# The finest recurrence level without differences and with factors copied into PSUM; low parts of the recurrence's weight tiles half on VectorE

## The chip, the cores and the metric

One NeuronCore of one Trainium2 chip runs the whole program. The time is the device time of one execution in microseconds (us). The engines are TensorE (PE), VectorE (DVE), ScalarE (ACT), GpSimd (POOL) and SyncE (SP, which issues DMA). Each takes its instructions in order; they wait for each other through semaphores.

## The reference

Two layers on 512 tokens of width 1024, all in float32: a latent attention (layer 0) and a gated linear recurrence (layer 1, `_hgrn2`), each followed by an expert layer (`_peer`) that takes most of the time. The change concerns the recurrence alone:

```python
f = lb + (1.0 - lb) * jax.nn.sigmoid(f_pre.astype(jnp.float32))
log_f = jnp.log(f)
k = 1.0 - f
...
b = jnp.cumsum(lfc, axis=2)
o_inter = jnp.einsum('bhtd,bhde->bhte', qc * jnp.exp(b), state)
diff = b[:, :, :, None, :] - b[:, :, None, :, :]
decay = jnp.where(causal, jnp.exp(jnp.where(causal, diff, 0.0)), 0.0)
a = jnp.einsum('bhtd,bhsd,bhtsd->bhts', qc, kc, decay)
o_intra = jnp.einsum('bhts,bhse->bhte', a, vc)
...
o = o * lax.rsqrt(jnp.mean(o * o, axis=-1, keepdims=True) + NORM_EPS)
o = o.reshape(B, S, E) * out_norm.astype(jnp.float32) * jax.nn.silu(g_pre.astype(jnp.float32))
```

There are 8 heads (128 channels each). The output of a head is normed, so its sign can be set back in the gain that follows.

## The kernel before

**The stream of weights.** All weights pass as tiles of 128 x 1024 through a ring of 4 slots (`RING`). SP loads a tile to `w_raw`. ScalarE rounds it to `w_hi` (`high`, L700), and the rest `w_raw - w_hi` goes to `w_lo`: by POOL (`lows`, L612) or by VectorE (`low`, L1389), as `low_by_dve` says. Before the change VectorE makes low parts only in the expert layers. A product of weights and activations is three matmuls (`three`, L1640 to L1642: high x high, and the two with a low part); PE waits for a tile's low part with `wait_low`. The tiles concerned are `hg_g` 0 to 7 (gate projection, one for each head) and after them `hg_out` 0 to 7 (output projection); `hg_g` + 8 is `hg_out` 0.

**The recurrence.** The 512 steps are worked on in 4 chunks of 128. Inside a chunk the decayed product of queries and keys is split into 8 levels: level 0 is the diagonal, and level p = 1 to 7 pairs blocks of m = 128 >> p steps with the blocks beside them; in level 7 m is 1. For each head h there are 8 slots k, so n = 8h + k runs from 0 to 63, and every engine has a loop over n:

- POOL (`take_diff`): the differences of the cumulated log decay against a block's edge, into one of two buffers `diff`. L646 in slot 0, L651 in slots 1 to 7. In slot 0 `head_roots(h - 2)` (L663, L666) follows, and low parts (L612) at n = 6, 9, 11, 16, 24, 32, 40, 48, 56, the last three for `hg_out` 0 to 2. After the loop come `head_roots` 6 and 7 and the low part of `hg_out` 3.
- ScalarE (`level_exp`): exponentials of the differences into one of two PSUM banks (`scaling`), L971 in slot 0, L976 (keys) and L977 (queries) in the others. Between them: the copy of the transposed keys `kdT` (L1016) and `next_high` (L700) in slot 5, the gate's tanh (L951) in slot 4, squares (L983) in slot 6, `head_scaled` (L991) in slot 1, the decay (L963) after slot 7.
- VectorE (`scale_level`): keys and queries times these factors (L1489 in slot 0; L1499, L1500 else) into `xx`, also two buffers. `mask_level` (L1511, L1519) takes PE's result of two slots before out of PSUM. Then `gate_silu` (L1538), `gated` (L1544), `states` (L1528, L1530) and q times decay (L1568) in slot 7. Head 7 has three `gated_low` (L1551) besides.
- PE follows the list `recurrence()`: per head level 0 (L1941), the transposes of the decayed keys (`kd`, L1925), levels 1 to 7 (L1939), the chunk states (`st`, L1950) after level 3, which need `kdT`, the transposes `turn` (L1958), 8 parts of a gate tile (three matmuls each) strewn between, and values and output of the head before (L1985, L1994) after level 1. A level waits for `xx` and for the mask step that frees its PSUM bank (two are in turn). After the last head: parts of the output projection in the order `hg_out` 0 and 1 (all by L1640 to L1642), then 2 and 3, then `turn` 7.

In level 7 both key and edge are the same step, so the key's factor is exp(0) = 1 and the query's is f itself, computed by difference and exponential.

## Time and profile before

| | us |
|---|---|
| median of 3 runs | 2929.11 |
| lowest, highest | 2926.78, 2932.37 |
| the profiled execution | 2927.46 |
| its span (first to last instruction) | 2925.2 |
| PE busy | 2893.8 |
| VectorE busy | 2364.2 |
| POOL busy | 1285.6 |
| ScalarE busy | 1194.7 |
| recurrence, level 0 of head 0 to the end of head 7 | 1550.68 to 1661.63 |

The busy times are of the whole program; the recurrence is under 4% of it. A busy PE includes matmuls that overlap one another, so short waits between them may not be seen as idle time. Times of rows are from the start of the span. What ended an idle time is inferred from semaphores.

### The profile page before, as it was taken

The numbers are of one execution on the slowest core, as the hardware profiler recorded it, in microseconds if no ns is written. First come the engines' busy times: TensorE is split into PE (matmuls) and PEld (weight loads), VectorE is DVE, ScalarE is ACT, GpSimd is POOL, SyncE is SP. The second block draws the span as 40 slices with busy tenths as digits, with TensorE's granted clock in tenths as the row PEclk, the third lists the DMA queues.
The fourth block names the chain that finished last, engine by engine and source line by source line (L and its number), as shares of the span: only waits on it lengthen the run. The fifth ranks groups of instructions, "written<-read, shape, count | busy, mean of one in ns | idle before, by whom it ended". The sixth has DMA issues, their size and how long they took to land.

```text
span 2925.2 us, 43270 instructions
## 1 busy us (share of the span) xinstructions
PE 2893.8 (99%) x15746; PEld 2581.3 (88%) x15746; DVE 2364.2 (81%) x4466; ACT 1194.7 (41%) x1928; POOL 1285.6 (44%) x764
## 2 busy tenths in 40 slices
PE   8999999999999999999999999999999999999998
PEld 7678999999998888888887788999999998888887
DVE  7537999999878888888356758999998978888887
ACT  6543334444433333333436543334444433333333
POOL 4133565334444444442348643664334444444441
PEclk9999999999999999999999999999999999999999
DMA  4122568999999999998321032669999999999995
GB/s 152 37 100 90 165 183 311 367 377 363 372 379 398 361 362 361 359 357 320 107 95 57 30 116 91 199 197 366 365 379 351 381 396 378 361 358 364 360 362 212
DMA packets 346146, 799.96 MB, mean 273 GB/s; under 512 B 27984, under 2 KB 192080, under 8 KB 345680
## 3 DMA queue, kind: packets, MB, share of 16 engines
q1 hardware_dynamic: 235200, 478.32, 47.2%
q0 software_dynamic: 73728, 268.47, 24.1%
q10 hardware_dynamic: 37008, 50.41, 4.7%
q8 instruction: 127, 2.08, 0.3%
q14 instruction: 83, 0.68, 0.1%
HBM read 694.33 MB, written 102.76 MB: 272 GB/s over the span
## 4 chain that ended last, share of the span: by engine, by line
PE 94%; POOL 2%; ACT 2%; DVE 1%; issue 0%; DMA 0%; DVEq 0%; SPq 0%; ACTq 0%
PE PS L1640 29%; PE PS L1642 29%; PE PS L1641 29%; PE PS L1861 3%; PE PS L1840 1%; POOL w_lo L612 1%; POOL arena L651 1%; PE PS L1770 1%; PE PS L1771 1%; PE PS L1817 1%; DVE resid L1114 1%; ACT arena L713 0%; ACT PS L976 0%; ACT PS L977 0%; PE PS L1805 0%
## 5 line engine op out<-in xcount | busy, mean ns | idle before, releaser
L700 ACT ACTIVATE w_hi<-w_raw 128x1024 fp32r<-128x1024 f32 x607 | 641.4, 1058 | 758.2 <-PE PS L1642 691.1
L1640 PE MATMUL PS<-x_hi,w_hi 128*128 128x384 f32 (+1 forms) x2564 | 897.5, 350 | 0.0
L1642 PE MATMUL PS<-x_hi,w_lo 128*128 128x384 f32 (+1 forms) x2564 | 886.3, 346 | 0.0
L1641 PE MATMUL PS<-x_lo,w_hi 128*128 128x384 f32 (+1 forms) x2564 | 885.2, 345 | 0.0
L1640 PE MATMUL PS<-w_hi,x_hi 128*128 128x512 f32 x1744 | 679.7, 390 | 1.7 <-POOL w_lo L612 0.9
L1642 PE MATMUL PS<-w_hi,x_lo 128*128 128x512 f32 x1744 | 678.6, 389 | 0.0
L1641 PE MATMUL PS<-w_lo,x_hi 128*128 128x512 f32 x1744 | 678.5, 389 | 0.0
L623 POOL DMA_INDIRECT arena<-in_v_t,arena x256 | 427.0, 1668 | 557.4 <-DVE resid L1412 527.5
L612 POOL TENSOR_TENSOR w_lo<-w_raw,w_hi 128x1024 fp32r<-128x1024 f32 x167 | 414.7, 2489 | 493.3 <-ACT w_hi L700 493.2
L1389 DVE TENSOR_TENSOR w_lo<-w_raw,w_hi 128x1024 fp32r<-128x1024 f32 x440 | 536.6, 1219 | 97.1 <-ACT w_hi L700 92.0
L623 POOL DMA_INDIRECT arena<-in_u_rows,arena x256 | 363.9, 1421 | 509.9 <-DVE arena L1396 455.6
L1642 PEld LDWEIGHTS PS<-x_hi,w_lo 128*128 128x128 f32 x2564 | 481.2, 188 | 21.2
L1641 PEld LDWEIGHTS PS<-x_lo,w_hi 128*128 128x128 f32 x2564 | 481.8, 188 | 18.3 <-issue 0.5
L1640 PEld LDWEIGHTS PS<-x_hi,w_hi 128*128 128x128 f32 x2564 | 481.7, 188 | 17.7 <-issue 0.5
L1640 PEld LDWEIGHTS PS<-w_hi,x_hi 128*128 128x128 f32 x1744 | 327.4, 188 | 70.5 <-POOL w_lo L612 1.3
L1641 PEld LDWEIGHTS PS<-w_lo,x_hi 128*128 128x128 f32 x1744 | 327.4, 188 | 68.0
L1642 PEld LDWEIGHTS PS<-w_hi,x_lo 128*128 128x128 f32 x1744 | 327.4, 188 | 68.0
L871 ACT ACTIVATE arena<-PS 128x384 f32<-128x384 f32 x256 | 125.9, 492 | 639.5 <-PE PS L1642 631.3
L1412 DVE SCALAR_TENSOR_TENSOR resid<-arena,resid 128x1024 f32<-128x1024 f32 x256 | 327.1, 1278 | 1.3
L1396 DVE SCALAR_TENSOR_TENSOR arena<-arena 128x1024 f32<-128x1024 f32 x256 | 306.9, 1218 | 0.4
L1429 DVE TENSOR_TENSOR x_lo<-arena,x_hi 128x384 fp32r<-128x384 f32 x256 | 144.6, 565 | 165.8 <-ACT x_hi L902 160.1
L1423 DVE TENSOR_TENSOR arena<-arena 128x384 f32<-128x384 f32 x256 | 141.0, 551 | 2.9 <-DMA arena<-acts_dram 2.9
(203 smaller groups left out, 2314.1 us busy)
## 6 DMA issues: line engine op xcount, KB each, us to landing
w_raw<-in_u_t SPq DMA_DIRECT2D x256, 512.0 KB
w_raw<-in_v_t SPq DMA_DIRECT2D x256, 512.0 KB
acts_dram<-arena ACTq DMA_DIRECT2D x256, 192.0 KB
gates_dram<-arena SPq DMA_DIRECT2D x24, 2048.0 KB
arena<-acts_dram SPq DMA_DIRECT2D x256, 192.0 KB
arena<-gates_dram SPq DMA_DIRECT2D x64, 768.0 KB
w_raw<-in_hg_t SPq DMA_DIRECT2D x40, 512.0 KB
w_raw<-in_pq_t SPq DMA_DIRECT2D x32, 512.0 KB
```

What stands on the lines that cost most here:

```text
L612: pool.tensor_tensor(w_lo[:, n % RING, :], w_raw[:, n % RING, :], f32(w_hi[:, n % RING, :]), ALU.subtract).then_inc(pool_low, 1)
L623: pool.indirect_dma_start(row[k % ROWS], None, u_at if k < HK else v_at, bass.IndirectOffsetOnAxis(ap=at, axis=0))\
L700: act.activation(w_hi[:, slot, :], w_raw[:, slot, :], ACT.Copy).then_inc(hi_ready, 1)
L871: act.activation(act_st[:, c % RING, :], PS[:, c % 4, 0:D], ACT.Gelu).then_inc(gelu_done, 1)
L1389: dve.tensor_tensor(w_lo[:, n % RING, :], w_raw[:, n % RING, :], f32(w_hi[:, n % RING, :]), ALU.subtract).then_inc(dve_low, 1)
L1396: dve.scalar_tensor_tensor(r, r, 1.0, far_x, ALU.mult, ALU.mult, accum_out=far_act[:, k:k + 1]).then_inc(sem("dotted"), 1)
L1412: dve.scalar_tensor_tensor(resid[:, FAR, :], r, far_w[:, k:k + 1], resid[:, FAR, :], ALU.mult, ALU.add).then_inc(sem("far_added"), 1)
L1423: dve.tensor_tensor(product[:, c % RING, :].rearrange(tokens, t=HALF_TOK), act_ld[:, c % RING, :].rearrange(tokens, t=HALF_TOK), gate_ld[: ...
L1429: dve.tensor_tensor(product_at(x_lo, c), product[:, c % RING, :].rearrange("p (t n) -> p t n", n=P), product_at(f32(x_hi), c), ALU.subtrac ...
L1640: pe.matmul(ps, wh, xh, start=start, stop=False)
L1641: pe.matmul(ps, wh, xl, start=False, stop=False)
L1642: return pe.matmul(ps, wl, xh, start=False, stop=stop)
```

## The change

Level 7 (slot 7) no longer uses a difference or an exponential. The kernel keeps k with its sign turned, gk = f - 1. ScalarE copies gk into the PSUM bank of factors, keys' and queries' part. VectorE copies the keys' part to `xx`, and makes the queries' part as (factor + 1) x q, which is f x q. The turned sign passes through the head's output and is set back by a negative gain. POOL's loop takes 7 differences a head instead of 8; the buffers of `diff` alternate by 7h + k. In head 0 ScalarE copies `kdT` in slot 3 instead of slot 5. The low parts of `hg_g` 3, 5, 7 and of `hg_out` 1 are made by VectorE in slots n = 11, 27, 43, 59; POOL makes those of `hg_g` 2, 4, 6 and `hg_out` 0 at n = 8, 20, 36, 44, and that of `hg_out` 2 after the loop, behind both `head_roots`. The function `low` is moved out of `experts`, unchanged.

```diff
@@ -132,6 +132,8 @@
 def low_by_dve(n):
 
 
+    if BASE["hg_g"] <= n < BASE["pq1"]:
+        return n - BASE["hg_g"] in (3, 5, 7, 9)
     return any(BASE[f"u{k}"] + FIRST_DVE_LOW <= n < BASE[f"v{k}"] + NKEYS for k in range(2))
 
 
@@ -637,9 +639,9 @@
             def take_diff(n):
 
 
-                h, k = divmod(n, 8)
+                h, k = divmod(n, LEVELS)
                 if n >= 2:
-                    pool.wait_ge(sem("level_exp"), n - 1)
+                    pool.wait_ge(sem("level_exp"), (n - 2) // LEVELS * 8 + (n - 2) % LEVELS + 1)
                 d = diff[:, n % 2, :]
                 half, b = SEQ // 2, gb[:, h, :]
                 if k == 0:
@@ -668,17 +670,18 @@
             pool.wait_ge(sem("cumulated"), HEADS)
             pool.memset(minus_half, -0.5).then_inc(sem("exponent_made"), 1)
             pool.wait_ge(sem("exponent_made"), 1)
+            low_at = {8: 2, 20: 4, 36: 6, 44: 8}
             for n in range(8 * HEADS):
-                take_diff(n)
-                if n % 8 == 0 and n >= 16:
-                    head_roots(n // 8 - 2)
-                if n in (6, 9, 11):
-                    lows(BASE["hg_g"] + n // 3, BASE["hg_g"] + n // 3 + 1) if n < 11 else                         lows(BASE["hg_g"] + RING, BASE["hg_g"] + RING + 1)
-                elif n >= 16 and n % 8 == 0:
-                    lows(BASE["hg_g"] + RING + n // 8 - 1, BASE["hg_g"] + RING + n // 8)
+                h, k = divmod(n, 8)
+                if k < LEVELS:
+                    take_diff(LEVELS * h + k)
+                if k == 0 and h >= 2:
+                    head_roots(h - 2)
+                if n in low_at:
+                    lows(BASE["hg_g"] + low_at[n], BASE["hg_g"] + low_at[n] + 1)
             head_roots(HEADS - 2)
             head_roots(HEADS - 1)
-            lows(BASE["hg_out"] + RING - 1, BASE["u1"] + FIRST_GATHER)
+            lows(BASE["hg_out"] + 2, BASE["u1"] + FIRST_GATHER)
             gathers(1)
 
 
@@ -964,15 +967,20 @@
 
             def level_exp(n):
                 h, k = divmod(n, 8)
-                act.wait_ge(sem("level_diff"), n + 1)
                 scaling_used(act, n - 2)
-                d = diff[:, n % 2, :]
+                d = diff[:, (LEVELS * h + k) % 2, :]
+                if k < LEVELS:
+                    act.wait_ge(sem("level_diff"), LEVELS * h + k + 1)
                 if k == 0:
                     act.activation(scaling(n), d, ACT.Exp).then_inc(sem("level_exp"), 1)
                     return
 
                 m = P >> k
                 by_part = scaling(n).rearrange("p (w s b m) -> p w s b m", w=2, s=2, m=m)
+                if k == LEVELS:
+                    act.activation(by_part[:, 0], level_keys(gk[:, h, :], m), ACT.Copy)
+                    act.activation(by_part[:, 1], level_queries(gk[:, h, :], m), ACT.Copy).then_inc(sem("level_exp"), 1)
+                    return
                 act.activation(by_part[:, 0], level_keys(d, m), ACT.Exp, scale=-1.0)
                 act.activation(by_part[:, 1], level_queries(d, m), ACT.Exp).then_inc(sem("level_exp"), 1)
 
@@ -1011,10 +1019,11 @@
                 for k in range(8):
                     if 8 * h + k >= 2:
                         level_exp(8 * h + k)
-                    if k == 5:
+                    if k == (5 if h else 3):
                         ready(act, ("kd", h))
                         free(act.activation(kdT.rearrange("p a b -> p (a b)"), PSb(("kd", h)), ACT.Copy),
                              ("kd", h))
+                    if k == 5:
                         if h < HEADS - 1:
                             next_high(BASE["hg_g"] + h)
                     if k == 6 and h >= 1:
@@ -1106,6 +1115,12 @@
                     free(dve.scalar_tensor_tensor(x_lo[:, c, :], PSb(("xT", k, c)), gain[:, g:g + 1],
                                                   f32(x_hi[:, c, :]), ALU.mult, ALU.subtract),
                          ("xT", k, c))
+
+            def low(n):
+
+                dve.wait_ge(hi_ready, n + 1)
+                dve.tensor_tensor(w_lo[:, n % RING, :], w_raw[:, n % RING, :], f32(w_hi[:, n % RING, :]),
+                                  ALU.subtract).then_inc(dve_low, 1)
 
             def add_to_resid(name, t):
                 for n in (2 * t, 2 * t + 1):
...
@@ -1461,12 +1470,12 @@
             norm(2, "v0")
 
             out_gain = gain[:, G_AT["out"]:G_AT["out"] + HEADS]
-            chain(dve.tensor_scalar(out_gain, out_gain, 0.5 * P ** 0.5, None, ALU.mult))
+            chain(dve.tensor_scalar(out_gain, out_gain, -0.5 * P ** 0.5, None, ALU.mult))
             for h in range(HEADS):
                 was_freed(dve, ("hg_f", h))
                 chain(dve.tensor_scalar(gb[:, h, :], gb[:, h, :], lbt[:, 3, h:h + 1], lbt[:, 1, h:h + 1],
                                         ALU.mult, ALU.add))
-                chain(dve.tensor_scalar(gk[:, h, :], gb[:, h, :], -1.0, 1.0, ALU.mult, ALU.add))
+                chain(dve.tensor_scalar(gk[:, h, :], gb[:, h, :], 1.0, None, ALU.subtract))
                 dve.tensor_scalar(gb[:, h, :], gb[:, h, :], SMALLEST_F, None, ALU.max)\
                    .then_inc(sem("forget"), 1)
             dve.wait_ge(sem("mask_in"), 16)
@@ -1496,6 +1505,12 @@
                 factor = d.rearrange("p (w s b m) -> p w s b m", w=2, s=2, m=m)
                 keys = xx[:, x % 2, 0:SEQ // 2].rearrange("p (b s m) -> p s b m", s=2, m=m)
                 queries = xx[:, x % 2, SEQ // 2:SEQ].rearrange("p (s b m) -> p s b m", s=2, m=m)
+                if k == LEVELS:
+                    dve.tensor_copy(keys, factor[:, 0])
+                    dve.scalar_tensor_tensor(queries, factor[:, 1], 1.0,
+                                             level_queries(gq[:, h, :], m), ALU.add, ALU.mult)\
+                        .then_inc(sem("level_x"), 1)
+                    return
                 dve.tensor_tensor(keys, level_keys(gk[:, h, :], m), factor[:, 0], ALU.mult)
                 dve.tensor_tensor(queries, level_queries(gq[:, h, :], m), factor[:, 1], ALU.mult)\
                    .then_inc(sem("level_x"), 1)
@@ -1551,6 +1566,7 @@
                 dve.tensor_tensor(x_lo[:, h, :], gq[:, h, :], f32(x_hi[:, h, :]), ALU.subtract)\
                    .then_inc(sem("gated_low"), 1)
 
+            low_in_slot = {11: 3, 27: 5, 43: 7, 59: 9}
             for n in range(8 * HEADS):
                 h, k = divmod(n, 8)
                 if k == 0 and n >= 2:
@@ -1569,6 +1585,8 @@
                        .then_inc(sem("q_decayed"), 1)
                 if k == 5 and h >= 2:
                     gated(h - 2)
+                if n in low_in_slot:
+                    low(BASE["hg_g"] + low_in_slot[n])
                 if (h, k) in ((7, 1), (7, 3), (7, 5)):
                     gated_low(k // 2)
             mask_level(8 * HEADS - 2)
```

## Rows read from the trace of the kernel before

**Rows 1.** The page: busy us of each engine (share of the span) x instructions.

```profile
PE 2893.8 (99%) x15746; PEld 2581.3 (88%) x15746; DVE 2364.2 (81%) x4466; ACT 1194.7 (41%) x1928; POOL 1285.6 (44%) x764
```

**Rows 2.** PE's waits in the whole span: total us, times, longest us.

```profile
PE PS L1950 <- ACT arena L1016: 2.7, 2, 1.4
```

**Rows 3.** Stages by head (0, 1, 3, 7): length, busy PE PEld DVE ACT POOL, clock.

```profile
1550.68:1563.49 12.81, 11.11 (x72) 9.53 (x70) 10.24 (x23) 6.11 (x15) 10.08 (x7) 1.00 0.13 43
1563.49:1578.24 14.75, 12.77 (x84) 11.15 (x85) 12.73 (x29) 7.98 (x25) 13.59 (x12) 1.00 0.23 75
...
1592.13:1605.98 13.85, 13.66 (x90) 11.48 (x89) 11.86 (x30) 9.65 (x31) 12.31 (x12) 1.00 0.14 40
...
1647.47:1661.63 14.16, 11.97 (x79) 9.98 (x80) 13.34 (x31) 9.99 (x35) 8.57 (x9) 1.00 0.10 36
```

**Rows 4.** Timeline of PE in head 3: start, us, what.

```profile
1601.38 0.60 PE L1939 MATMUL PS<-arena 128*128 128x128 f32 x4
1601.74 0.48 PE L1640 MATMUL PS<-x_hi,w_hi 128*128 128x512 f32 x1
...
1602.29 0.40 PE L1642 MATMUL PS<-x_hi,w_lo 128*128 128x512 f32 x1
1602.76 0.71 PE L1939 MATMUL PS<-arena 128*128 128x128 f32 x4
```

**Rows 5.** Timeline of POOL, end of head 3 and start of head 4.

```profile
1602.31 2.39 POOL L612 TENSOR_TENSOR w_lo<-w_raw,w_hi 128x1024 fp32r<-128x1024 f32 x1
1604.65 3.56 POOL L651 TENSOR_TENSOR arena<-arena 128x512 f32<-128x512 f32 x3
1608.61 4.10 POOL L651 TENSOR_TENSOR arena<-arena 128x512 f32<-128x512 f32 x4 [0.39 <-ACT PS L977]
```

**Rows 6.** Timeline of ScalarE, levels 1, 2 and 5 of head 4, then kdT.

```profile
1606.19 0.39 ACT L976 ACTIVATE PS<-arena 128x256 f32<-128x256 f32 x1 [3.13 <-POOL arena L651]
...
1607.82 0.40 ACT L976 ACTIVATE PS<-arena 128x256 f32<-128x256 f32 x1
...
1610.85 0.38 ACT L976 ACTIVATE PS<-arena 128x256 f32<-128x256 f32 x1
...
1611.46 0.58 ACT L1016 ACTIVATE arena<-PS 128x512 f32<-128x512 f32 x1
```

**Rows 7.** Timeline of VectorE in head 4.

```profile
1606.91 0.42 DVE L1499 TENSOR_TENSOR arena<-arena,PS 128x256 f32<-128x256 f32 x1 [0.50 <-ACT PS L977]
...
1607.59 0.73 DVE L1519 COPY_PREDICATED arena<-mask_bits,PS 128x256 f32<-128x256 uint16 x1
...
1611.90 0.42 DVE L1499 TENSOR_TENSOR arena<-arena,PS 128x256 f32<-128x256 f32 x1 [0.97 <-PE PS L1939]
```

**Rows 8.** Timeline of ScalarE and PE in head 0.

```profile
1551.57 0.60 PE L1925 MATMUL PS<-const,arena 128*128 128x128 f32 x4
...
1554.50 0.60 ACT L951 ACTIVATE arena<-PS 128x512 f32<-128x512 f32 x1 [3.41 <-PE PS L1642]
...
1555.61 0.59 ACT L1016 ACTIVATE arena<-PS 128x512 f32<-128x512 f32 x1
...
1556.34 0.91 PE L1950 MATMUL PS<-arena 128*128 128x128 f32 x6 [1.43 <-ACT arena L1016]
```

**Rows 9.** POOL and VectorE in head 1; lines L1389, L1528: ns min/median/max.

```profile
1574.62 2.38 POOL L612 TENSOR_TENSOR w_lo<-w_raw,w_hi 128x1024 fp32r<-128x1024 f32 x1
...
1575.05 2.50 DVE L1568 TENSOR_TENSOR arena<-arena 128x512 f32<-128x512 f32 x1
...
L1389 DVE TENSOR_TENSOR w_lo<-w_raw,w_hi x440: 1212/1218/1246, 454.2 to 2904.1; 128x1024 fp32r<-128x1024 f32 x147
...
L1528 DVE COPY arena<-PS x8: 275/281/303, 1558.8 to 1658.3; 128x128 f32<-128x128 f32 x8
```

**Rows 10.** Timeline after head 7, POOL and PE.

```profile
1669.18 2.38 POOL L612 TENSOR_TENSOR w_lo<-w_raw,w_hi 128x1024 fp32r<-128x1024 f32 x1
...
1671.61 0.50 PE L1640 MATMUL PS<-w_hi,x_hi 128*128 128x512 f32 x1 [0.88 <-POOL w_lo L612]
```

More of the change, by code:

```diff
@@ L1384, in make_onehots @@
                        .then_inc(onehots, 1)
-                def low(n):
-                    dve.wait_ge(hi_ready, n + 1)
-                    dve.tensor_tensor(w_lo[:, n % RING, :], w_raw[:, n % RING, :], f32(w_hi[:, n % RING, :]),
-                                      ALU.subtract).then_inc(dve_low, 1)
                 def far_dot(k):
```

## Prediction

> **What bounds the kernel now.** I read the page's busy line first: TensorE (PE) is busy for 2893.8 of 2925.2 us [rows 1], so nearly all of the program is a TensorE stream that this change doesn't touch. The waits of PE come next: the largest entry inside the recurrence is L1950's for ScalarE's kdT copy, 2.7 us in two waits [rows 2]. The change leaves PE's instructions as they are. It can move only the time in which PE waits in the recurrence.
>
> That time is found with a table of stages, cut where PE starts level 0 of a head (L1941) [rows 3]. Head 0 takes 12.81 us, head 1 14.75, head 3 13.85 (heads 2 to 6, five of them, differ by under 0.1), head 7 14.16, all at a granted clock of 1.00. A modelled PE row hides short waits, so I compare starts. A level group (L1939) that is not waited for starts 0.36 us before the next 512-column matmul (1601.38 to 1601.74). The matmul at 1602.29 should hand over after 0.23 us, but the next L1939 starts at 1602.76, 0.47 later, and needs 0.47 instead of 0.36 us itself [rows 4]. So a wait costs 0.24 + 0.11 us and no idle is shown. Walking one steady head (1592.13 to 1605.98) this way gives 0.38 at level 1, 0.35 at level 6, and 0.33 in four small ones, 1.06 us together: PE's floor for a head is 12.8 us. Five steady heads hold 5.3 us; the shown idle of heads 0, 1, 7 and the tail, with the hidden part ahead of each, about 10 more. Some 16 us (0.5%) is the most that any change of this kind could win.
>
> What PE waits for in a steady head is a ring of engines. POOL works off a low part (2.39 us) and then the differences [rows 5]. ScalarE's exponential of level 1 waits 3.13 us for the first of these [rows 6]; VectorE then waits 0.50 us for ScalarE before it scales level 1, and masks level 7 of the head before at 1607.59 (0.73 us), which frees PE's bank for level 1. It waits again, 0.97 us at 1611.90, for PE's level 2 [rows 7]. From there to the next level 0 VectorE runs without a break but for drains, so it is the second bound, 0.50 us behind POOL.
>
> **The change, part by part.** (a) POOL loses the level-7 difference of each head (1.03 us, from four in 4.10 [rows 5]) and four of its low parts at 2.39. It also issues the others elsewhere: at slots 8, 20, 36, 44 instead of right ahead of each head's level-1 difference. In a head with no low part the 3.13 us wait goes, VectorE's 0.50 goes with it, and the mask of level 7 comes early enough for PE's 0.38 to go. Next late is VectorE's unbroken stretch, and PE's level 6 wait stays. A steady head without a POOL low part (3 and 6) therefore gains 0.4 to 0.5: 0.95 for both.
>
> (b) Head 0: ScalarE copies kdT at level 3 instead of after level 5, ahead of the gate's tanh. The copy is at 1555.61 now, behind the tanh, which ScalarE reaches after 3.41 us of idle, and PE's L1950 starts at 1556.34, after 1.43 of idle of its own. The transposes that the copy needs end at 1552.2 (1551.57 + 0.60) [rows 8], so it can end at 1552.8, and PE can take L1950 straight after level 3. It isn't free: ScalarE now stands at kd(0) until 1552.2 with a tile's high part and the exponential of level 4 queued behind it. The latter ended at 1551.1 (the tanh's start less its idle) and now ends at about 1554.4; the 3.41 us absorb it. VectorE takes level 4 half a microsecond later, and PE needs that only after L1950, so the cover holds. I take 1.5 us here, and 0.25 for the product of q and the decay, which in heads 0 and 1 is blocked behind a POOL low part (2.50 us in head 1 [rows 9]; free it should be under 0.7, since twice its size takes 1.22, below): 1.75.
>
> (c) Head 1 has three low parts of POOL in or just ahead of it now, and none after. It loses the blocked 2.50, the late exponential behind it and the second L1950 wait; walked through at the row times it ends at PE's floor of 12.55 (no turn(h-2) in it): gain 2.2.
>
> (d) Heads 2, 4, 5 carry a POOL low part between the differences of levels 4 and 5. In a steady head's times, ScalarE's second exponential frees the buffer at 1607.82 + 0.7, some 1.3 earlier after (a), so at 1607.2. POOL would then do difference 4 until 1608.35, the low part until 1610.75 and difference 5 until 1611.8. The exponential of level 5, at 1610.85 now, comes at 1612.0, and the kdT copy behind it on ScalarE, at 1611.46 now, at 1612.6 [rows 6]. PE's L1950 waits for that copy with everything of PE queued behind it. That costs 1.15 against now, of which later slack gives back most of 0.8: each of these heads is 0.35 to 0.4 longer than now, 1.1 for three. Were the exponential not late it would be -0.4 each, were the low part fully on the path +1.6: the ends are -1.2 and +4.8.
>
> (e) VectorE gets four low parts, at level 3 of heads 1, 3, 5, 7. One takes 1.22 us (440 rows of the same operation [rows 9]). In heads 1 and 3 it sits where VectorE waits 0.97 for PE now, and 1.3 after (a), so the wait hides it: nothing. In head 5 it meets POOL's low part and waits for it, 0.3. Head 7 has no such wait, since three gated_low steps fill it: +1.2, less 0.5 from (a) and 0.2 that PE gives back: +0.5. If that cover fails altogether each costs up to 1.2, and up to 1.0 more behind a difference of POOL.
>
> (f) Level 7: ScalarE's two exponentials become two copies of 256 columns from the same strides. No row has a copy of that shape into PSUM; the nearest are the 256-column exponential at 0.39 us and kdT's copy, 0.58 for 512 columns, so 0.29 to 0.39 [rows 6]. I take 0.39, no change; ScalarE is not the bound. On VectorE the key product becomes a copy from PSUM. L1528, 128 columns, takes 0.281 against 0.42 for 256 columns in L1499 [rows 9, 7], so by size 256 cost the same; at best 0.14 x 8 = 1.1 us of VectorE go. I take nothing. The sign of k is carried through and cancelled in the gain: same instructions.
>
> (g) The tail. Today the low part of hg_out tile 2 is made at slot 56, in head 7, and only tile 3's is made after head_roots(7): POOL's at 1669.18 for 2.38, and PE's first matmul of tile 3 starts at 1671.61, 0.88 idle [rows 10]. After the change both stand behind head_roots(7), which waits for the last head's squares. Tile 2's is ready at 1671.6, tile 3's at 1673.95. PE, in order, stops at 1669.2 for 2.4 us, does 1.4 us of tile 2, and stops again. Tile 3 starts at 1674.0 instead of 1671.6: +2.4. Nothing else of PE can pass, and DMA loads behind the two tiles have over 5 us of slack.
>
> **The sum.** -1.75 - 2.2 - 0.95 + 1.1 (heads 2, 4, 5) + 0.3 + 0.5 + 2.4 = -0.6 us. The profiled execution took 2927.46 us, 2.26 more than its span; it becomes 2926.9. The median of the runs lies 1.65 above it, so 2928.5. A measurement of this kernel can tell some 0.2%, 5.9 us, from no change.
>
> One rule speaks against (e). The row shows VectorE's product with two SBUF sources at 2.50 us, ending 0.5 after a POOL low part that had begun 0.43 before it [rows 9]. The Trainium skill (SBUF — State Buffer, Who interferes with whom) says that such an instruction and a GpSimd one that reads SBUF share a port pair as an exclusive lock: the later one is blocked until the first ends. By that rule, the trace agrees, every new VectorE low part can block a difference or be blocked by one; this is the price of up to 1.0 in (e).
>
> **The rivals.** *The collision of (d) takes the place of the old wait* (slower side): the exponential of level 5 is late by the whole low part. Price: 4.8 instead of 1.1, and 2 more where VectorE's low parts block or wait for differences: 2928.5 + 3.7 + 2 = 2934. It decides when (d) and (e) exceed the 3.95 of (b) and (c) less the tail's 2.4. For: POOL has one pair of buffers, so difference 5 can't run ahead. Against: POOL has 3 us of slack per head after (a). To be over +0.2% it must also lose head 0's gain.
>
> *The gain of (a) reaches every head*: the late difference is hidden by VectorE's stretch, heads 2, 4, 5 gain 0.4. Sum -0.6 - 2.3 - 0.3 = -3.2: 2925.9. For: VectorE takes level 5 only behind level 4 (1611.90 [rows 7]), a mask and the gate. Against: PE's L1950 waits for the copy behind that exponential, wherever VectorE is.
>
> *Head 0 doesn't gain*, since ScalarE stands at kd(0) and its queue comes late: +1.5, 2930.0.
>
> *The tail doesn't cost* (tile 2 is covered by something I don't see): -2.4, 2926.1; with the rival above 2923.5. Against: the order of POOL is plain in the code.
>
> **How the numbers follow.** Forecast 2928.5 as it stands, chance 0.45; the second rival 0.14; head 0 0.14; no tail cost 0.07; the collision 0.20, of which 0.09 beyond +0.2%. The bounds of (d) alone reach from -2.3 to +3.7 around the forecast; with the 2.8 us by which the runs of the kernel before lie around their median, of which about 1.5 stay in a median (2926.2 - 1.5, 2932.2 + 1.5), the range is 2924.7 to 2933.7. Within 0.2% of before (2923.3 to 2935.0): 0.86. Faster: 0.05, mostly the second and fourth rivals together. Slower: 0.09, the far part of the collision.
>
> **What the profile would show.** Right: no wait of ScalarE for POOL at level 1; L1950 of head 0 near 1554.7; head 1 under 13 us; heads 3 and 6 at 13.3 to 13.5; PE idle before L1950 in heads 2, 4, 5; and in the tail two L1640 waits for POOL's low parts, 2.2 and 0.9 us. Wrong: the even heads no longer than the odd ones, VectorE low parts above 1.3 us, or hg_out tile 2 not waited for. The prediction falls if PE's idle in the recurrence shrinks by over 6 us or grows.

## The result, and the profile after

The changed kernel takes 2932.6 us (median; 2929.8 to 2938.8), the kernel before 2929.1. The ratio is 1.0013, with a 95% interval of 1.0007 to 1.0019: 3.5 us slower, by 2.1 to 5.6. That is inside the range (2924.7 to 2933.7) and inside the 0.2% that I gave 0.86, but I had forecast 0.6 us faster, and the interval excludes that. 4.1 us have to be found. The wide upper side of the range came from the bounds of (d); (d) kept its forecast and other things filled that space, so the hit of the range is luck.

The page of after says nothing of it. Its busy line, as [rows 1] for before:

```profile
PE 2893.0 (99%) x15746; PEld 2583.2 (88%) x15746; DVE 2368.6 (81%) x4470; ACT 1195.5 (41%) x1928; POOL 1264.6 (43%) x752
```

POOL lost 21 us and 12 instructions (8 differences, 4 low parts), VectorE gained 4 instructions and 4 us, PE is as busy as before. The stages show more. The table of stages of after, cut where PE starts level 0 of a head (line L1959 now); the columns are those of [rows 3]; the last line goes from turn 6 to turn 7 (L1976), which is the tail:

```profile
1549.94:1561.69 11.75, 11.27 (x71) 9.60 (x70) 9.57 (x23) 7.27 (x16) 7.71 (x6) 1.00 0.13 45
1561.69:1574.65 12.96, 12.81 (x84) 11.30 (x85) 12.78 (x30) 9.87 (x31) 9.58 (x10) 1.00 0.14 42
1574.65:1588.96 14.31, 13.06 (x90) 11.53 (x89) 12.16 (x30) 9.89 (x31) 11.17 (x11) 1.00 0.12 39
1588.96:1602.43 13.47, 13.36 (x89) 11.44 (x89) 13.08 (x31) 9.87 (x31) 9.13 (x10) 1.00 0.13 39
1602.43:1616.77 14.34, 13.07 (x89) 11.58 (x88) 12.18 (x30) 10.03 (x32) 11.23 (x11) 1.00 0.11 38
1616.77:1633.62 16.85, 14.62 (x90) 13.10 (x90) 14.64 (x33) 10.38 (x33) 12.04 (x11) 0.90 0.20 64
1633.62:1646.95 13.33, 11.73 (x80) 9.71 (x78) 10.63 (x28) 9.85 (x31) 8.29 (x9) 1.00 0.00 1
1646.95:1661.82 14.87, 12.13 (x80) 10.03 (x80) 14.56 (x32) 8.62 (x30) 5.55 (x6) 1.00 0.13 36
1661.82:1675.57 13.75, 10.89 (x54) 8.60 (x55) 3.81 (x6) 5.16 (x17) 5.90 (x4) 1.00 0.16 46
```

Beside before and beside what the steps of the prediction come to (us):

| | h0 | h1 | h2 | h3 | h4 | h5 | h6 | h7 | tail | sum |
|---|---|---|---|---|---|---|---|---|---|---|
| before | 12.81 | 14.75 | 13.89 | 13.85 | 13.86 | 13.82 | 13.81 | 14.16 | 11.47 | 122.4 |
| by my steps | 11.06 | 12.55 | 14.3 | 13.35 | 14.2 | 14.5 | 13.35 | 14.7 | 13.87 | 121.9 |
| after | 11.75 | 12.96 | 14.31 | 13.47 | 14.34 | 16.85 | 13.33 | 14.87 | 13.75 | 125.6 |

The recurrence became 3.2 us longer, nearly all of the 3.5. Six of the nine stages are within 0.2 us of my steps, heads 0 and 1 fall short by 0.7 and 0.4 us of gain, and head 5 alone is 2.35 us too long. It is also the only line whose clock column isn't 1.00.

PE's waits from the first level 0 to turn 7 of after (total us, times, longest), those over 0.5 in total:

```profile
PE PS L1968 <- ACT arena L1024: 4.8, 3, 2.2
PE PS L1957 <- DVE arena L1534: 3.1, 5, 0.9
PE PS L1658 <- POOL w_lo L614: 2.9, 2, 2.2
PE PS L1959 <- DVE arena L1534: 1.0, 2, 0.5
```

The wait for kdT was 2.7 us in two waits, in heads 0 and 1 [rows 2]; now it is 4.8 in three, and these are heads 2, 4 and 5: the change has moved the wait and made it longer. The wait for POOL's low parts in the tail went from 0.88 [rows 10] to 2.9. Added up, PE's shown waits over these stages grew from 8.2 to 12.3 us.

Two of the signs that I had named as speaking against me are there: PE's idle grew, and all four of VectorE's low parts took over 1.3 us (1.58, 1.58, 1.90 and 1.41). The signs for me are there too: L1968 of head 0 came 4.07 us after level 0 (1554.01), head 1 took 12.96, heads 3 and 6 took 13.47 and 13.33, PE idled before L1968 in heads 2, 4 and 5, and twice in the tail. Most of the walk through the heads was right.

**Head 5.** Timeline of VectorE, POOL, ScalarE and PE of after in head 5:

```profile
1620.65 1.90 DVE L1122 TENSOR_TENSOR w_lo<-w_raw,w_hi 128x1024 fp32r<-128x1024 f32 x1
...
1619.10 2.38 POOL L614 TENSOR_TENSOR w_lo<-w_raw,w_hi 128x1024 fp32r<-128x1024 f32 x1
1621.43 3.02 POOL L653 TENSOR_TENSOR arena<-arena 128x512 f32<-128x512 f32 x2
...
1623.55 0.39 ACT L984 ACTIVATE PS<-arena 128x256 f32<-128x256 f32 x1 [2.70 <-POOL arena L653]
...
1624.18 0.58 ACT L1024 ACTIVATE arena<-PS 128x512 f32<-128x512 f32 x1
...
1624.90 0.91 PE L1968 MATMUL PS<-arena 128*128 128x128 f32 x6 [2.23 <-ACT arena L1024]
...
1627.95 0.63 PE L1660 MATMUL PS<-x_hi,w_lo 128*128 128x512 f32 x1
1628.38 0.63 PE L1658 MATMUL PS<-x_hi,w_hi 128*128 128x512 f32 x1
```

Read it from the top. VectorE's low part starts at 1620.65 while POOL's (1619.10 to 1621.48) is under way and takes 1.90 us instead of 1.22. It is still running when POOL comes to its differences, and these two take 3.02 instead of 2.04 (heads 2 and 4). So the exponential of level 5 waits 2.70 us, kdT comes behind it at 1624.18, and PE stands for 2.23 us. So far this is my step (d) with (e) on top. Then comes what I had not thought of: PE's matmuls of 512 columns, which start 0.23 us apart elsewhere, start 0.43 apart. The stages around that place, columns as above:

```profile
1622.67:1624.90 2.23, 0.00 (x1) 0.03 (x1) 2.10 (x6) 1.35 (x4) 2.23 (x3) 1.00 0.60 125
...
1626.00:1629.30 3.30, 3.30 (x13) 2.81 (x12) 2.53 (x7) 3.02 (x13) 1.76 (x3) 0.50 0.28 109
1629.30:1633.62 4.32, 4.32 (x27) 3.76 (x26) 3.61 (x9) 2.27 (x8) 2.63 (x3) 1.00 0.01 2
```

The granted clock is 0.50, the lower level of 1.2 GHz, in the stretch from 1626.0 to 1629.3, about 1 us behind the end of the idle of 2.23 us; up to 1625.5 and from 1629.3 on it is 1.00, which is 2.4 GHz. The profile of before has no such place in the recurrence.

**The tail.** Timeline of POOL and PE of after behind head 7:

```profile
1669.34 4.68 POOL L614 TENSOR_TENSOR w_lo<-w_raw,w_hi 128x1024 fp32r<-128x1024 f32 x2
...
1671.74 0.50 PE L1658 MATMUL PS<-w_hi,x_hi 128*128 128x512 f32 x1 [2.20 <-POOL w_lo L614]
1674.07 0.50 PE L1658 MATMUL PS<-w_hi,x_hi 128*128 128x512 f32 x1 [0.66 <-POOL w_lo L614]
```

Here I was right: both low parts stand behind `head_roots`, PE stops twice, and turn 7 comes at 1675.57 instead of 1673.10.

### The profile page after: what moved, and what is told of

Same layout as the page of the kernel before. It is cut to its first block, busy times and chain, and to the rows that moved or that the text cites. A ratio compares the mean times of both kernels' runs of the same rounds, so it can differ in the third digit from the quotient of the medians.

```text
span 2929.1 us, 43254 instructions
## 1 busy us (share of the span) xinstructions
PE 2893.0 (99%) x15746; PEld 2583.2 (88%) x15746; DVE 2368.6 (81%) x4470; ACT 1195.5 (41%) x1928; POOL 1264.6 (43%) x752
## 4 chain that ended last, share of the span: by engine, by line
PE 95%; DVE 2%; ACT 1%; POOL 1%; issue 1%; DMA 0%; DVEq 0%; SPq 0%; ACTq 0%
PE PS L1658 29%; PE PS L1660 29%; PE PS L1659 29%; PE PS L1879 3%; PE PS L1858 1%; PE PS L1788 1%; PE PS L1835 1%; PE PS L1789 1%; DVE resid L1129 1%; POOL w_lo L614 0%; ACT arena L716 0%; PE PS L1957 0%; DVE arena L1534 0%; PE PS L1823 0%; PE PS L1668 0%
## 5 line engine op out<-in xcount | busy, mean ns | idle before, releaser
L1122 DVE TENSOR_TENSOR w_lo<-w_raw,w_hi 128x1024 fp32r<-128x1024 f32 x444 | 543.4, 1224 | 100.0 <-ACT w_hi L703 93.5
L614 POOL TENSOR_TENSOR w_lo<-w_raw,w_hi 128x1024 fp32r<-128x1024 f32 x163 | 404.8, 2488 | 492.8 <-ACT w_hi L703 492.7
```

The source lines that it names most:

```text
L614: pool.tensor_tensor(w_lo[:, n % RING, :], w_raw[:, n % RING, :], f32(w_hi[:, n % RING, :]), ALU.subtract).then_inc(pool_low, 1)
L1122: dve.tensor_tensor(w_lo[:, n % RING, :], w_raw[:, n % RING, :], f32(w_hi[:, n % RING, :]), ALU.subtract).then_inc(dve_low, 1)
```

## The experiments

The theories: (T1) the loss sits in the POOL low part between the differences of levels 4 and 5, in head 5 in its meeting with VectorE's, and in the tail; what remains of the change wins. (T2) The half clock in head 5 is a loss of its own that follows PE's idle. (T3, rival) Something that the whole change brings, the copies into PSUM or VectorE's four low parts, costs everywhere, and its place in head 5 is chance. All kernels below compute the whole result. For each the stages of its profile are given as in the table above.

**The changed kernel again.** No edit.

> The changed kernel once more, unaltered, timed and profiled. Two theories of why it is about 3.5 us slower than before. Theory 1 (a collision and the clock): in head 5 VectorE's low part in slot 43 and POOL's in slot 44 block each other, difference 5 comes late, PE idles 2.2 us and then runs 3.4 us at half its clock, so head 5 takes 16.9 us instead of 13.8. Then a second profile shows PE's L1968 of head 5 again waiting over 2 us; the half clock shows again if the idle alone causes it. Theory 2 (the low parts of VectorE cost as such): head 5's length is work on VectorE, and the clock was a chance of that one profile; then head 5 comes out near 14.5 to 15.5 here. The tail's wait for POOL (2.2 and 0.7 us) is the same in both. Time against before: 1.0005 to 1.0015 by theory 1, 1.000 to 1.0008 by theory 2.

Stages: 11.74 12.95 14.31 13.47 14.34 16.88 13.34 14.86, tail 13.76. Not one differs from after by over 0.03 us, the half clock in head 5 included. Time 2930.45 against 2928.59, ratio 1.0007 (0.9998 to 1.0016). So stages can be compared to a tenth of a microsecond between single profiles of the recurrence, while the time of a whole run can't be told to 2 us.

**POOL's low part of head 5 three slots later.**

```diff
-low_at = {8: 2, 20: 4, 36: 6, 44: 8}
+low_at = {8: 2, 20: 4, 36: 6, 47: 8}
```

> The changed kernel, POOL's low part of hg_out 0 moved from slot 44 to slot 47, where no difference of this head stands behind it. Theory 1: the collision is gone, ScalarE's kdT copy comes in time, PE doesn't idle before L1968 in head 5, the clock stays at full and head 5 takes 13.3 to 13.6 us instead of 16.9: 3.3 us less than the changed kernel, about level with before. Theory 2 (VectorE's own 1.2 us is what costs): head 5 stays over 14.5 us and the gain is under 1 us.

Head 5 takes 13.49 instead of 16.85, all other stages are the same to 0.1. Time 2927.92, ratio 0.9997 (0.9988 to 1.0006). One tile's low part in one slot was worth 3.4 us. In this head of that kernel the two engines still get in each other's way, POOL and then VectorE:

```profile
1622.13 3.35 POOL L614 TENSOR_TENSOR w_lo<-w_raw,w_hi 128x1024 fp32r<-128x1024 f32 x1
...
1621.67 1.59 DVE L1122 TENSOR_TENSOR w_lo<-w_raw,w_hi 128x1024 fp32r<-128x1024 f32 x1
```

3.35 instead of 2.38 and 1.59 instead of 1.22, and PE has no shown wait in the whole head. So a meeting as such need not cost PE anything. I read it so that what decides is whether a difference that somebody waits for stands behind the two.

**VectorE's low part of head 5 two slots earlier.**

```diff
-low_in_slot = {11: 3, 27: 5, 43: 7, 59: 9}
+low_in_slot = {11: 3, 27: 5, 41: 7, 59: 9}
```

> The changed kernel, VectorE's low part of hg_g 7 moved from slot 43 to slot 41, before POOL's low part begins in slot 44, which stays. Theory 1: head 5 becomes like heads 2 and 4, which have a POOL low part alone: 14.3 us, PE idles about 1.3 us before L1968, the clock stays at full; 2.5 us less than the changed kernel. Theory 2: VectorE does the same work, so head 5 stays near its length of the unaltered kernel. If the half clock comes with 1.3 us of idle too, head 5 takes about 16 us.

I had expected head 5 to become like heads 2 and 4 (14.3). It takes 15.33. POOL, then VectorE, in this head of that kernel:

```profile
1619.66 3.35 POOL L614 TENSOR_TENSOR w_lo<-w_raw,w_hi 128x1024 fp32r<-128x1024 f32 x1
...
1618.90 1.89 DVE L1122 TENSOR_TENSOR w_lo<-w_raw,w_hi 128x1024 fp32r<-128x1024 f32 x1
```

VectorE's now meets a difference first (1.89) and then holds up POOL's low part (3.35). So the collision was moved, not avoided. PE's wait before L1968 is 1.62 instead of 2.23 us, with 0.30 one level earlier, and head 5 keeps the full clock. In this kernel it falls in the tail instead, after the wait of 2.20 us there, and the tail takes 14.49 instead of 13.75. Time 2930.22, ratio 1.0009 (1.0000 to 1.0018).

**The tail as before: POOL makes hg_out 2 in slot 55.**

```diff
-low_at = {8: 2, 20: 4, 36: 6, 44: 8}
+low_at = {8: 2, 20: 4, 36: 6, 44: 8, 55: 10}
...
-            lows(BASE["hg_out"] + 2, BASE["u1"] + FIRST_GATHER)
+            lows(BASE["hg_out"] + 3, BASE["u1"] + FIRST_GATHER)
```

> The changed kernel, POOL's low part of hg_out 2 made in slot 55 (head 6) instead of behind both head_roots. The tail as in the prediction: from turn 6 to turn 7 PE takes 11.5 us instead of 13.75, the 2.2 us wait for a POOL low part goes and one of 0.9 us stays, 2.3 us less than the changed kernel. The rival: PE's time in the tail is bound by turn 7's chain, and the wait moves to another place: less than 1 us is won.

The tail takes 11.46, so the 2.3 us are this one tile's place. But head 6 takes 14.30 instead of 13.33. In slot 55 POOL waits 1.83 us for ScalarE's high part, and its first differences of head 7 come late by that and by the low part (1644.92). VectorE's product of q and the decay (1645.99) meets them and takes 1.54 us instead of the 0.68 of after, and level 0 of head 7 waits 1.38 us for the mask behind it. That one place gives back 1.0 of the 2.3 us. Time 2929.14, ratio 1.0002 (0.9993 to 1.0011).

This kernel also bears on T2. The edit lies behind head 5, which has the same code, the same collision and the same idle, and keeps its clock. Timeline of PE:

```profile
1626.70 0.91 PE L1968 MATMUL PS<-arena 128*128 128x128 f32 x6 [2.24 <-ACT arena L1024]
1627.44 0.60 PE L1976 MATMUL PS<-const,arena 128*128 128x128 f32 x4
```

The stage of the 3 us behind it, columns as above:

```profile
1627.88:1630.85 2.97, 2.97 (x19) 2.59 (x18) 2.48 (x7) 2.95 (x13) 1.49 (x3) 1.00 0.16 65
```

Head 5 takes 15.35 with the full clock and 16.85 and 16.88 with the half clock, in front of the same work. From L1968 to the second L1957 behind it, it is 3.01 us here (1626.70 to 1629.71) and 4.60 in after (1624.90 to 1629.50). So the 3.0 us that head 5 lost against before are 0.5 from POOL's low part (as heads 2 and 4), 1.0 from the collision and 1.5 from the clock.

**All of POOL's low parts in slot 7** (n = 23, 39, 47), in two series on two chips.

```diff
-low_at = {8: 2, 20: 4, 36: 6, 44: 8}
+low_at = {8: 2, 23: 4, 39: 6, 47: 8}
```

> The changed kernel with POOL's low parts of hg_g 4 and 6 and hg_out 0 in slot 7 of their heads (n = 23, 39, 47) instead of slot 4 (20, 36, 44). Theory: a POOL low part between differences 4 and 5 makes difference 5, the kdT copy and so L1968 of PE late. Heads 2 and 4, 14.3 us with it, then take about 13.5 us, as head 5 did once its low part stood in slot 47; L1968 isn't waited for. 1.7 us less than the run with slot 47 alone. The rival: heads 2 and 4 are long because head 3's pace is handed on (even heads have no VectorE low part, so something else is late); then they stay over 14 us.

> The kernel with all POOL low parts in slot 7 once more, unaltered, beside the mended one on the same chip. In its first profile the clock fell in the tail and in the expert layer though no wait there was longer than in the changed kernel. Theory: which stretch falls varies from execution to execution, the lengths of heads 0 to 7 do not (11.75, 12.96, 13.4 to 13.46 for heads 2 to 6, 14.86). The rival: the fall is tied to the program; then the tail is 14.6 us again and the expert layer falls in the same place.

Heads 2 to 6 all take 13.40 to 13.47. Against after that is -0.9, -0.9 and -3.4 us in heads 2, 4 and 5. Heads 3 and 5, with a low part on VectorE (1.58 us each), take 13.44 to 13.47, heads 2, 4 and 6 without one 13.40 to 13.47. Times 2926.81 (ratio 0.9996, 0.9987 to 1.0005) and 2926.23 (0.9989, 0.9980 to 0.9998). In both profiles the clock falls in the tail, in or right behind the wait of 2.2 us. I had expected the place of a fall to change from one execution to the next; the fall in the tail came again, a second one in an expert layer did not. Stages of the second one's tail:

```profile
1664.30:1666.50 2.20, 0.01 (x1) 0.00 (x0) 0.00 (x0) 1.02 (x4) 2.20 (x2) 1.00 0.00 0
1666.50:1669.90 3.40, 3.38 (x8) 2.69 (x9) 0.00 (x0) 0.00 (x0) 2.29 (x1) 0.52 0.47 164
```

It costs only 0.6 us there (14.37 against 13.77 with the same wait and the full clock, in the kernel with slot 47), and 0.8 in the first profile (14.60): PE, at half speed, reaches the second tile when its low part is ready, so the wait of 0.66 us isn't paid besides.

**Level 7 without differences, alone.** The kernel before, with the level-7 part of the change only (7 differences a head, the two copies on ScalarE, the COPY and (factor + 1) x q on VectorE, the turned sign).

```diff
-                take_diff(n)
+                if n % 8 < LEVELS:
+                    take_diff(LEVELS * (n // 8) + n % 8)
...
+                if k == LEVELS:
+                    act.activation(by_part[:, 0], level_keys(gk[:, h, :], m), ACT.Copy)
+                    act.activation(by_part[:, 1], level_queries(gk[:, h, :], m), ACT.Copy).then_inc(sem("level_exp"), 1)
+                    return
```

> The kernel before with the level-7 part of the change alone: seven differences a head, copies into PSUM, the turned sign; low parts and the kdT copy as before. Theory: POOL's ring was only 0.50 us longer than VectorE's, and 1.03 us go from it, so each of heads 2 to 6 falls to 13.4 to 13.5 us without any low part moved; 2 to 2.5 us less than before in all, ratio about 0.9992. The rival: the low part right before difference 1 is what made it late, and dropping a difference behind it helps nothing: heads stay at 13.8.

Stages: 12.36 14.18 13.93 13.91 13.91 13.89 13.87 14.21, tail 11.44. Time 2928.96, ratio 1.0001 (0.9992 to 1.0010). My theory of 13.4 to 13.5 falls and its rival holds: steady heads don't gain, they even lose 0.05; heads 0 and 1 gain 0.45 and 0.57. Timeline of POOL and of ScalarE at the end of head 4, as [rows 5, 6] for before:

```profile
1613.27 0.23 POOL L663 TENSOR_SCALAR arena<-arena 128x4 f32<-128x4 f32 x1 [2.12 <-ACT arena L989]
1613.58 1.04 POOL L666 TENSOR_TENSOR arena<-arena 128x4 f32<-128x4 f32 x1
1614.59 2.38 POOL L612 TENSOR_TENSOR w_lo<-w_raw,w_hi 128x1024 fp32r<-128x1024 f32 x1
1616.93 3.58 POOL L651 TENSOR_TENSOR arena<-arena 128x512 f32<-128x512 f32 x3
...
1618.54 0.39 ACT L982 ACTIVATE PS<-arena 128x256 f32<-128x256 f32 x1 [3.26 <-POOL arena L651]
```

POOL has the microsecond of the removed difference, but waits 2.12 us in it for the squares, and the low part and difference 1 come no sooner. ScalarE still waits 3.26 us. In steady heads the 0.4 us are won by taking the low part out from in front of difference 1, and not by the shorter chain of differences.

**The low parts, alone.** The change, with level 7 and the kdT copy as before. The edit against after, without the level-7 lines of ScalarE and VectorE:

```diff
-                if k < LEVELS:
-                    take_diff(LEVELS * h + k)
+                take_diff(n)
...
-                    if k == (5 if h else 3):
+                    if k == 5:
...
-                    if k == 5:
```

> The kernel before with the low parts moved as in the change (four on VectorE, POOL's at 8, 20, 36, 44, hg_out 2 behind the roots); level 7 by differences and kdT as before. Theory: the moved low parts carry the whole loss, so with POOL doing 8 differences a head this is the slowest: heads 2, 4 and 5 at 14.3 to 15.5 us (near 17 if the clock falls), the tail at 13.8, 3 to 5 us over before. The rival: head 1 gains as much here as in the changed kernel (1.8 us) since it comes from the low parts, and the rest evens out: within 2 us of before.

Stages: 12.37 13.18 14.43 13.49 14.41 16.89 13.32 15.82, tail 14.36. Time 2933.71, ratio 1.0015 (1.0006 to 1.0024). Heads 2, 4 and 5 lose as in after, head 3 and head 6 win as in after, without the level-7 part. The whole loss comes with the low parts. The half clock is there too, in head 5 and in the tail. Head 7 takes 0.95 more than in after, though the level-7 part alone gains nothing there (14.21 against 14.16): it is worth something in head 7 only beside the moved low parts. That this is because VectorE and POOL are full there is argued, not shown.

**The early kdT, alone.**

```diff
-                    if k == 5:
+                    if k == (5 if h else 3):
...
+                    if k == 5:
```

> The kernel before with the kdT copy of head 0 in slot 3 as its only change. Theory: PE's 1.43 us wait before L1950 in head 0 goes and head 0 takes 11.4 to 11.8 us instead of 12.81; head 1 and the rest stay, so 1.0 to 1.4 us less than before in all, at the limit of what the timing shows. The rival: ScalarE standing at kd(0) delays the high part and level 4, and the time comes back in head 0 or 1: no gain.

Stages: 11.39 17.73 14.21 14.32 14.31 14.31 14.29 14.55, tail 11.45. Time 2932.78, ratio 1.0015 (1.0006 to 1.0024). Head 0 gains 1.42, close to my 1.5, and head 1 loses 3.0. Timeline of POOL in heads 0 and 1, and of PE in head 1:

```profile
1554.60 1.04 POOL L651 TENSOR_TENSOR arena<-arena 128x512 f32<-128x512 f32 x1 [3.76 <-ACT PS L977]
1555.60 2.40 POOL L612 TENSOR_TENSOR w_lo<-w_raw,w_hi 128x1024 fp32r<-128x1024 f32 x1
...
1560.96 2.84 POOL L612 TENSOR_TENSOR w_lo<-w_raw,w_hi 128x1024 fp32r<-128x1024 f32 x1
1563.76 2.11 POOL L651 TENSOR_TENSOR arena<-arena 128x512 f32<-128x512 f32 x2
1565.82 2.37 POOL L612 TENSOR_TENSOR w_lo<-w_raw,w_hi 128x1024 fp32r<-128x1024 f32 x1
...
1571.72 0.91 PE L1951 MATMUL PS<-arena 128*128 128x128 f32 x6 [3.00 <-ACT arena L1016]
```

The stage behind that wait:

```profile
1573.00:1576.40 3.40, 3.40 (x12) 2.85 (x11) 1.98 (x6) 2.86 (x13) 3.00 (x4) 0.52 0.02 5
```

POOL waits 3.76 us for the exponential of level 4, which ScalarE does only behind the early copy. Against head 1's start (1562.26 here, 1563.49 before) its next two low parts begin at -1.3 and +3.6 us, where before they began at -3.7 and +1.2 (1559.84 and 1564.71). The differences of head 1 that ScalarE's exponentials need stand behind them, PE waits 3.00 us for kdT, and the clock is halved behind it. The 3.41 us of ScalarE's idle that I named as cover [rows 8] cover ScalarE, and not POOL. Why the steady heads of this kernel are 0.5 us longer I haven't followed up; it stays open.

**What the three experiments on slots point to.** POOL's low parts in slot 7, those of hg_out 2 and 3 before `head_roots(7)`, and none on VectorE in head 7.

```diff
-        return n - BASE["hg_g"] in (3, 5, 7, 9)
+        return n - BASE["hg_g"] in (3, 5, 7)
...
-            low_at = {8: 2, 20: 4, 36: 6, 44: 8}
+            low_at = {8: 2, 23: 4, 39: 6, 47: 8, 55: 9}
...
             head_roots(HEADS - 2)
+            lows(BASE["hg_out"] + 2, BASE["hg_out"] + 4)
             head_roots(HEADS - 1)
-            lows(BASE["hg_out"] + 2, BASE["u1"] + FIRST_GATHER)
+            lows(BASE["hg_out"] + 4, BASE["u1"] + FIRST_GATHER)
...
-            low_in_slot = {11: 3, 27: 5, 43: 7, 59: 9}
+            low_in_slot = {11: 3, 27: 5, 43: 7}
```

> The changed kernel with the three places mended: POOL's low parts in slot 7 of heads 2, 4, 5 and 6 (n = 23, 39, 47, and 55 for hg_out 1, which VectorE no longer makes in slot 59), those of hg_out 2 and 3 between head_roots(6) and head_roots(7). Theory: heads 2 to 6 at 13.4 to 13.5 us, head 7 at 13.6 to 14.2 without VectorE's low part, the tail at 10.6 to 11.5 without a wait for POOL; from level 0 of head 0 to turn 7 it takes 117 to 118.5 us against 122.4 before and 125.6 in the changed kernel. With full clock throughout 2924.5, ratio about 0.9985. The rival: the clock falls in some executions whatever the waits, and takes 1 to 3 us of this back: ratio 0.9993 or more.

Stages: 11.74 12.95 13.42 13.46 13.45 13.47 13.42 13.72, tail 10.28. Time 2921.36 against 2929.64, ratio 0.9974 (0.9964 to 0.9985): 8 us faster than before, and on the same chip 4.9 faster than the kernel with only the slots moved. I had expected 0.9985, with a tail of 10.6 to 11.5 us; this is 3 us better than that. Head 7, without VectorE's low part, takes 13.72 instead of 14.87; the tail is 4.1 us shorter than in the kernel with the slots alone (14.37), of which 2.2 are the wait, 0.7 the second wait that the full clock would have brought, and 0.6 the clock. The remaining 0.6 I can't place. Timeline of POOL in the tail:

```profile
1653.19 2.37 POOL L614 TENSOR_TENSOR w_lo<-w_raw,w_hi 128x1024 fp32r<-128x1024 f32 x1
1658.51 2.38 POOL L614 TENSOR_TENSOR w_lo<-w_raw,w_hi 128x1024 fp32r<-128x1024 f32 x1 [2.94 <-ACT w_hi L704]
1662.80 0.23 POOL L665 TENSOR_SCALAR arena<-arena 128x4 f32<-128x4 f32 x1 [1.91 <-ACT arena L992]
```

PE's waits in its recurrence, over 0.5 us in total:

```profile
PE PS L1958 <- DVE arena L1535: 2.3, 4, 0.6
PE PS L1960 <- DVE arena L1535: 1.0, 2, 0.5
```

Both low parts are done (1655.56 and 1660.89) before `head_roots(7)` even starts (1662.80), and PE waits for POOL or for kdT nowhere. Its shown waits are 3.8 us instead of 12.3, none over 0.65, and the clock is 1.00 throughout the recurrence. The tail is even 1.2 us shorter than before, which had made tile 3 behind `head_roots(7)` as well [rows 10].

The stage sums and the times go the same way, and lie within 2.2 us of each other. Against before the sums are +3.2 (again), 0.0 (slot 47), +2.6, +0.4, -1.1 and -1.2 (slot 7), -0.7, +5.8, +4.1 and -6.5 us; the medians against before on the same chip +1.9, -0.7, +1.6, +0.6, -1.9 and -3.4, +0.2, +5.0, +4.1 and -8.3.

## Why the prediction was wrong in its sign

**T1 holds, T2 in part, and T3 falls but for head 7.** The level-7 part alone costs nothing, and VectorE's low part costs nothing that shows in head 3 (with POOL's low parts in slot 7, heads 3 and 5 take what heads 2, 4 and 6 take). Low parts carry the loss in heads 2 and 4 (0.9 us together), head 5 (3.0) and the tail (2.3); a fourth place, which T1 didn't name, is VectorE's low part in head 7 (0.7 against before, and 1.15 less without it).

**The step that failed is (e) in head 5.** I put +0.3 on VectorE's low part meeting POOL's. The meeting cost 1.0: I let VectorE wait for POOL, and left out that POOL's next differences then wait for VectorE. That is the "up to 1.0 more behind a difference of POOL" which I had named as the bound of (e) if its cover failed, and had left out of head 5's term. That is 0.7 us of the miss. The Trainium skill (SBUF — State Buffer, Who interferes with whom) has the lock hold for the whole instruction and block whoever comes second; the rows agree at each meeting, 1.90 and 3.02, 3.35 and 1.59, 1.89 and 3.35 us. I cited that rule and priced only half of a meeting: one makes two engines late, one behind the other.

**The other 1.5 us of head 5 were no term at all.** I asked what PE's idle costs, and took it for the idle itself. In after, its repetition and the kernel with the low parts alone the clock fell behind it in head 5, and the next matmuls started 0.43 us apart instead of 0.23. The same idle of 2.2 us had a fall behind it in some kernels and not in others:

| place | wait of PE, us | clock behind it |
|---|---|---|
| head 5, after, again, low parts alone | 2.23, 2.24, 2.23 | half |
| head 5, hg_out 2 in slot 55 | 2.24 | full |
| tail, after and again; slot 47 | 2.20 | full |
| tail, VectorE's in slot 41; slot 7 twice; low parts alone | 2.20 | half |
| head 1, kdT alone | 3.00 | half |
| head 7, kdT alone | 1.37 | half |
| head 7, hg_out 2 in slot 55 | 1.38 | full |
| head 0, before, levels alone, low parts alone | 1.43 | full |

Where the clock fell it cost 1.5 us in head 5 and 0.6 to 0.8 in the tail. So T2 holds in this form: the fall is a price of its own, and each fall of the table has idle of PE ahead of it, but the idle alone doesn't settle that it comes. It was not the whole of the wrong sign either: with the full clock in head 5 the stages would come to 1.7 us more than before, where I had 0.6 less. The Trainium skill (TensorE: Matmul & The Clock Gate, The HAM clock gate) says that a gate passes only some of the clock's pulses, by how busy PE has recently been. The rows fit that, with 0.50 behind idle and 1.00 before it and after, and it would have called for a rival: where a change adds an idle of 2 us to PE, the price may be 1.5 us more. It would have had to stand at head 5, where (d) and (e) had together a late kdT, and at the tail, where I had forecast 2.2 us of idle myself.

**(b) and (c), heads 0 and 1: right in kind, 1.1 us short.** L1968 of head 0 comes 4.07 us after its level 0 (I had said 4.0; before it was 5.66), so the 1.5 are there. VectorE's product of q and the decay isn't free, though. VectorE in heads 0 and 1 of after:

```profile
1559.52 1.49 DVE L1584 TENSOR_TENSOR arena<-arena 128x512 f32<-128x512 f32 x1
1560.92 0.71 DVE L1534 COPY_PREDICATED arena<-mask_bits,PS 128x256 f32<-128x256 uint16 x1
...
1565.56 1.58 DVE L1122 TENSOR_TENSOR w_lo<-w_raw,w_hi 128x1024 fp32r<-128x1024 f32 x1
...
1572.79 1.08 DVE L1584 TENSOR_TENSOR arena<-arena 128x512 f32<-128x512 f32 x1
```

The low part that used to block it is gone, and three of POOL's differences (1558.38 to 1561.94) block it instead: 1.49 us, where I had under 0.7. The mask behind it frees the bank for head 1's level 0, which waits 0.48 us for it. The kernel with kdT alone bears this out for a part: there the product takes 0.76 us, level 0 of head 1 has no shown wait, and head 0 takes 11.39 instead of 11.75. So some 0.4 of the 0.7 missing in head 0 goes with this meeting; the other 0.3 has no source that I can show. In head 1 the 1.58 and the 1.08 instead of 1.22 and 0.7 are 0.7 us for 0.4 missing; that is read from the timeline, and no run took these two away. And (b)'s gain isn't one by itself: alone it gives a loss of 4 us. In the whole change, where head 1 has fewer low parts of POOL, head 1 doesn't pay for it, and I had added the two as if they were independent. The sum was not hurt by this.

**(a): right size, one of two reasons empty.** Heads 3 and 6 are shorter by 0.38 and 0.48, as said. I put it down to POOL's list being shorter by a difference and to the low part being gone from ahead of difference 1. The level-7 part alone shows that the difference contributes nothing in steady heads, and the low parts alone show that moving them gives all of it.

**(d): right.** Heads 2 and 4 are 0.42 and 0.48 longer (I said 0.35 to 0.4), and PE idles 1.25 and 1.27 us before L1968 in them. With these low parts in slot 7 they gain 0.4 to 0.5 instead. The rival that the gain of (a) reaches every head is thus real as a kernel, only not as this one.

**(f): right.** The copy from PSUM on VectorE takes 0.42 us for 256 columns, as the product did, and ScalarE's copies 0.42 against 0.39. **Head 7** was +0.7 instead of +0.5; VectorE's low part took 1.41 instead of 1.22 there. **(g): right,** 2.28 instead of 2.4, with waits of 2.20 and 0.66 against my 2.2 and 0.9.

By terms: 0.7 and 0.4 (heads 0 and 1), 0.3 (heads 2, 3, 4), 2.35 (head 5), 0.2 (head 7), -0.1 (head 6 and tail) make 3.8 us, and the miss was 4.1. Of the rivals the collision came nearest, in its mechanism in one head of three only: I had priced it at 2934 with chance 0.20, and 2932.6 was in between. The forecast had put nearly every unknown at or near its lower bound: the blocked instructions at their free duration, (e) with two of its four at nothing, the clock not at all. Terms that all lean one way were the sign to look for. The size of the miss is less sure than its sign: the repetition of the changed kernel lay 1.9 us over before in time, though its stages came to the same 3.2.

## What to carry to other kernels

A low-priority piece of work should be put where nobody waits for what stands behind it in its queue: the same 2.4 us of POOL cost 0.9 us between the differences of levels 4 and 5 and nothing in slot 7 of heads 2, 4 and 5, where in head 5 it even met VectorE's. The slot alone is no guarantee: hg_out 2 in slot 7 of head 6 had to wait for its high part and cost 1.0 us there, hg_out 1 in the same slot cost nothing (13.42). Where two engines block each other, price both of them and the next consumer of each. And where a change adds some 2 us of idle to PE in one piece, put down the idle, and the idle with 1.5 us of slow matmuls behind it, as two cases.

## What the runs showed of the hardware that was not expected

The granted clock was halved after idle of 2.2 us, and behind the same idle it was not in other kernels whose work around it was the same. In head 5 the idle ended at 1624.90, 1624.74 and 1626.20 where the clock fell, and at 1626.70 where it didn't. In head 5 that decided 1.5 us, more than the collision itself. With kdT alone a wait of only 1.37 us had a fall behind it, while one of 1.38 at the same place of another kernel had none. The profile of the first kernel with slot 7 has another, 6.8 us long, in an expert layer, where PE had stood for 3.78 us without a releaser in the trace; it is not in the second profile of the same kernel. What decides whether the clock falls can't be told from these runs.

Meetings of POOL and VectorE went in chains. In three of them an instruction of POOL was first, VectorE's low part second and POOL's next third, and both later ones got longer: 1.90 and then 3.02 us (after, head 5), 1.89 and 3.35 (slot 41), 1.59 and 3.35 (slot 47), against 1.22 for the low part on VectorE, and 2.04 for two differences and 2.38 for the low part on POOL. So one meeting took 1.3 to 1.7 us from the two engines together.
